# Forty-eight modulation weight tiles start earlier in the weight stream, and two paired reductions are drawn together

## The reference

```
mod   = silu(c)     @ w_ada + b_ada      # w_ada: 1024 x 6144
mod_c = silu(c_ctx) @ w_ada + b_ada      # only its first 2 x 1024 columns are used
sh1, sc1, g1, sh2, sc2, g2 = split(mod, 6)
h_lat = rms_norm(x, norm_mix) * (1 + sc1) + sh1
h_ctx = rms_norm(ctx, norm_mix) * (1 + csc1) + csh1
... gated linear attention, long convolution, x = x + g1 * (... @ w_out), MLP with sh2, sc2, g2
```

## Time and profile before

| | us |
|---|---|
| median of 3 runs | 1745.04 |
| lowest, highest | 1741.37, 1745.97 |
| the profiled execution | 1745.97 |
| its span | 1744.2 |
| TensorE busy | 1663.2 (95%) |
| VectorE, ScalarE, GpSimd busy | 769.8, 670.2, 710.0 |

### The profile page before, as it was taken

One profiled execution on the slowest core, in us unless ns is written; L12 is line 12 of the kernel. 1 busy time (PEld: TensorE's weight loads), 2 busy tenths in 40 slices (PEclk: granted clock), 3 DMA queues, 4 the chain that ended last, 5 costly groups with the idle time before them and its releaser, 6 DMA issues.

```text
span 1744.2 us, 19877 instructions
## 1 busy us (share of the span) xinstructions
PE 1663.2 (95%) x8208; PEld 1360.9 (78%) x8208; DVE 769.8 (44%) x1083; ACT 670.2 (38%) x966; POOL 710.0 (41%) x333
## 2 busy tenths in 40 slices
PE   5899999999999899999999999989989899999997
PEld 5787888788878687888887757678968688888885
DVE  4635997565654333443432645653262421111113
ACT  6543333333322342444444353236633443232322
POOL 4834343343434434333333325342412365464642
PEclk9999999999999899999999999999999999999999
DMA  6323344333435222323222222121201132222221
GB/s 224 133 84 127 140 160 153 140 130 111 142 120 179 77 93 87 96 96 97 96 89 98 76 106 75 47 84 65 73 1 48 61 109 97 97 97 97 97 85 48
DMA packets 51953, 175.98 MB, mean 101 GB/s; under 512 B 6284, under 2 KB 6924, under 8 KB 51352
## 3 DMA queue, kind: packets, MB, share of 16 engines
q1 hardware_dynamic: 51864, 174.73, 29.4%
HBM read 169.44 MB, written 2.12 MB: 98 GB/s over the span
## 4 chain that ended last, share of the span: by engine, by line
PE 84%; DVE 8%; ACT 4%; POOL 2%; issue 1%; DMA 1%; SPq 0%; DVEq 0%; ACTq 0%; POOLq 0%
PE banks L77 84%; DVE T L77 1%; ACT L77 1%; POOL wl L77 1%; DVE TM L77 1%; DVE X L77 1%; ACT R L77 1%; DVE Sc L77 1%; DVE ACC L77 0%; ACT wh L77 0%; DMA raw<-wst_dram 0%; DVE Y L77 0%; ACT T L77 0%; POOL HL L77 0%; DVE QG L77 0%
## 5 line engine op out<-in xcount | busy, mean ns | idle before, releaser
L77 POOL TENSOR_TENSOR wl<-raw,wh 128x1024 fp32r<-128x1024 f32 x246 | 610.2, 2488 | 672.4 <-ACT wh L77 672.4
L77 PE MATMUL banks<-HH,wh 128*128 128x512 f32 x1040 | 417.6, 402 | 16.1 <-ACT HH L77 9.0
L77 PE MATMUL banks<-HL,wh 128*128 128x512 f32 x1040 | 408.5, 393 | 0.1
L77 PE MATMUL banks<-HH,wl 128*128 128x512 f32 x1040 | 407.9, 392 | 0.0
L77 ACT ACTIVATE wh<-raw 128x1024 fp32r<-128x1024 f32 x246 | 257.4, 1053 | 380.8 <-PE banks L77 350.8
L77 PEld LDWEIGHTS banks<-HH,wh 128*128 128x128 f32 x1040 | 197.3, 190 | 64.4 <-issue 14.3
L77 PEld LDWEIGHTS banks<-HL,wh 128*128 128x128 f32 x1040 | 196.7, 189 | 44.6 <-DVE HL L77 2.3
L77 PEld LDWEIGHTS banks<-HH,wl 128*128 128x128 f32 x1040 | 197.3, 190 | 42.2 <-issue 2.6
L77 PE MATMUL banks<-wh,HH 128*128 128x256 f32 x448 | 128.7, 287 | 2.0 <-ACT QX L77 2.0
L77 PE MATMUL banks<-wl,HH 128*128 128x256 f32 x448 | 127.4, 284 | 0.0
L77 PE MATMUL banks<-wh,HL 128*128 128x256 f32 x448 | 127.4, 284 | 0.0
(11 more groups left out here) (285 smaller groups left out, 2553.8 us busy)
## 6 DMA issues: line engine op xcount, KB each, us to landing
raw<-wst_dram SPq DMA_DIRECT2D x294, 512.0 KB, 3.2
CB<-sums_dram SPq DMA_DIRECT2D x12, 256.0 KB, 3.0
D<-dec_dram SPq DMA_DIRECT2D x12, 256.0 KB, 2.6
X<-xT_dram SPq DMA_DIRECT2D x1, 2048.0 KB, 11.4
out_dram<-X SPq DMA_DIRECT2D x8, 256.0 KB
QS<-QX SPq DMA_DIRECT2D x24, 64.0 KB, 2.9
KSw<-KX SPq DMA_DIRECT2D x24, 64.0 KB, 2.0
MX<-memT_dram SPq DMA_DIRECT2D x2, 512.0 KB, 6.1
```

The costliest lines, as they stand in the source:

```text
L77: i = w[0](*w[1], **w[2])
```

## The change

The plan inserts two "ada" tiles after each of the four memory units. As there are 48 in all, every later one moves up, two per unit are given while p < 2 instead of p < 3, and the last stands four slots earlier. The c_ctx reduction of groups 0 and 1 is named for the same take as the other one.

```diff
--- before.py
+++ after.py
@@ -109,11 +109,13 @@
     plan.append(("f", "fox", 0, None))
     for cols in [4620, 5132 + 1536, 4876, 5132 + 1792]:
         pair("fox", 0, 8, (cols,))
+        ada(left.pop())
+        ada(left.pop())
     for p in range(6):
         for cols in (1536 + 256 * p, 256 * p, 3072 + 256 * p, 5132 + 256 * p):
             pair("fox", 0, 8, (cols,))
             ada(left.pop())
-            if p < 3:
+            if p < 2:
                 ada(left.pop())
     for n in range(4):
         for k in (12, 0, 4, 8):
@@ -314,7 +316,7 @@
             at_u = st["take"] + 4
             later.append((at_u, ada_reduce(targets[0][0], mod[:, 8 * g:8 * g + 8], P("bada", 8 * g, 8))))
             if g < 2:
-                later.append((at_u + 1, ada_reduce(targets[1][0], modc[:, 8 * g:8 * g + 8], P("bada", 8 * g, 8))))
+                later.append((at_u, ada_reduce(targets[1][0], modc[:, 8 * g:8 * g + 8], P("bada", 8 * g, 8))))
 
     def split_next():
         i = st["split"]
```

## The result

| | before | after |
|---|---|---|
| median of 6 runs each, us | 1745.51 | 1754.96 |
| lowest, highest | 1741.37, 1746.68 | 1748.91, 1759.13 |
| span of the profiled execution | 1744.2 | 1755.0 |

The ratio is 1.0053, 95% interval 1.0035 to 1.0072: slower by 0.53%. The forecast was 1752.0 with a range to 1757; the sign and the range held, the sum was too small.

The account below looks back on a forecast made before the run. The prediction took TensorE's own work and a few stalls to bound the kernel. Stall terms summed to +7.0 us on 1745.97, giving 1753.0 for the profiled execution and 1752.0 for the median, range 1745 to 1757.

Parts of the forecast that it names:

- The frame of the argument: Whole kernel: time is TensorE's own work and a few stalls; the edit adds no work, only changes stalls.
- What a `wl` costs a sum: VectorE's modulation sums beside GpSimd: the engines alternate, so a `wl` costs 2.15 us and an `OL` 1.1.
- The heads: Memory heads: group 0's sums delay the copies to `PT`; TensorE stalls 1.2, 1.2 and 2.6 us, 5.0 in all.
- Rival A: Memory heads: the sums slip into VectorE's idle time, +1.5 us in all, 1746.5 us; chance 0.30.
- `Kt`: Entry to the first head pair: VectorE's late `Kt` copy stalls TensorE 0.3 us.
- The reductions: First head pair: group 0's two reductions back to back wait for banks 6 and 7; stall 2.4 us.
- the high bound of 4.6 us: Upper bound on the stall at group 0's reductions: one `wl` in between, 2.15 us more.
- Group 1's pair: Second head pair: group 1's two reductions, with only two sums ahead, stall TensorE 0.6 us.
- `Vt`: Second head pair, at 246.69: TensorE's 1.27 us wait on `Vt` goes, −1.3 us.
- `Sc`: At 496.37: the 3.0 us wait on `Sc` keeps the same sums around it and stays.
- rival B: Stalls reaching 3.01 us, or a reduction meeting a `wl`, bring slow matmuls, 1.8 us each; about 1757 us; chance 0.17.
- Sum: All terms: 1.2 + 1.2 + 2.6 + 0.3 + 2.4 + 0.6 − 1.3 = +7.0 us.

Follow-up runs that it names:

- experiment 7: The kernel before with one modulation tile, instead of none, behind each of the four memory units: 1746.42 us, ratio 0.9998.
- experiment 3: The full change with group 0's c_ctx sums left out except the first, so half of `mod_c` is not computed: 1747.94 us, ratio 1.0020.
- experiment 8: The kernel before with head 11's transposes moved behind the second slot of the output projection, beside its attention product: 1743.23 us, ratio 0.9990.
- the later c_ctx reduction: The kernel before with the c_ctx reduction of groups 0 and 1 three takes after the other instead of one: 1743.45 us, ratio 0.9988.
- 4: The full change with ScalarE making both copies to `PT` in the first layer's four memory heads: 1749.80 us, ratio 1.0026.
- 1: Two kernels: new plan with the c_ctx reductions one weight slot later as before, 1749.15 us; kernel before with both reductions in the same slot, 1749.43 us.
- 2: The full change with the c_ctx reductions of groups 0 and 1 on banks 4 and 5 instead of 6 and 7: 1748.06 us, ratio 1.0020.
- 6: The full change with both reductions of groups 0 and 1 one weight slot later, still drawn together: 1778.66 us, ratio 1.0191.
- reductions alone: The kernel before, old plan, with the two reductions of groups 0 and 1 in the same weight slot: 1749.43 us, ratio 1.0028.
- the last kernel of 8: The kernel before with head 11's transposes later and the c_ctx reductions of groups 0 and 1 three slots behind the others: 1740.03 us, ratio 0.9972.

## Why the prediction came out as it did

- **The frame of the argument** (TensorE's own work and its stalls, no work added) held: every microsecond found is a wait, its restart, or matmuls at the lower clock.
- **What a `wl` costs a sum.** Predicted 2.15 us, seen 3.41 − 1.27 = 2.14; an `OL` 1.1 predicted, 2.33 − 1.28 = 1.05 seen. They alternate strictly. By the rule of the Trainium skill, page "SBUF — State Buffer", section "SBUF: two separate sides" (whoever starts first has the shared pair for the whole instruction), the sums would be 3.7 and 2.6 us long, an estimate from 2.40 and 1.30 us; the runs have the alternation, not the full lengths.
- **The heads.** Predicted 1.2 + 1.2 + 2.6 = 5.0; waited 0.89 + 0.54 + 1.72 = 3.15, and 3.9 with the restarts. The places were right, each wait 0.3 to 0.9 us shorter than I had reckoned, while the restarts, which the sum has at nothing, added 0.2 to 0.3 each. Rival A, sums in idle time, fell with the same rows; experiment 7 shows where it would have been true.
- **`Kt`.** 0.3 predicted, none. As `Kt` was on time, the lateness handed on to the reductions was less than supposed, and experiment 3, with VectorE on time, shows that it was not the point.
- **The reductions: the step that failed in size.** I took 2.4 us, on the ground that the last sum "starts just before a `wl`, as it did"; the wait was 4.17 us, and 5.8 with the slow matmuls and the restart. Before the sum had begun 0.27 us ahead of the `wl`; after it came 0.16 us behind. The `wl` follows the copy `wh`, and this waits for its tile's transfer. ScalarE's row before, and after:

```profile
162.48 1.06 ACT L77 ACTIVATE wh<-raw 128x1024 fp32r<-128x1024 f32 x1 [4.40 <-DMA raw<-wst_dram]
```

```profile
168.50 1.06 ACT L77 ACTIVATE wh<-raw 128x1024 fp32r<-128x1024 f32 x1 [5.02 <-DMA raw<-wst_dram]
```

  The transfer in turn needs a slot of the ring, which VectorE gives back with the last sum ahead of `Kt`. That sum ended at 158.64 and at 165.08, and SyncE issued at once:

```profile
158.67 0.81 SPq L77 DMA_DIRECT2D raw<-wst_dram  x2
```

```profile
165.11 1.28 SPq L77 DMA_DIRECT2D raw<-wst_dram  x3
```

  So a late VectorE moves the `wl` along with its own sums, and the order hangs on how long the transfer takes: `wh` began 3.84 us behind that sum's end before, and 3.42 after. The old plan has the dear order too, with VectorE on time. GpSimd and VectorE in the kernel with the later turn (experiment 8):

```profile
163.65 5.97 POOL L77 TENSOR_TENSOR wl<-raw,wh 128x1024 fp32r<-128x1024 f32 x2 [7.35 <-ACT wh L77]
```

```profile
163.95 3.42 DVE L77 SCALAR_TENSOR_TENSOR ada<-raw,scc,ada 128x1024 f32<-128x1024 f32 x1
```

  Of the five profiles with the old plan, two have the sum first (before and the later c_ctx reduction) and three the `wl`. Of the five with the new plan and VectorE's copy to `PT` ahead of the four sums, all have the `wl` first. "As it did" was thus one outcome of two in a single trace, and the row could not carry the term. What came is the case which I priced as the high bound of 4.6 us. Experiments 3 and 4 stand on the two sides of this race: 3.17 and 1.49 us waited.
- **Group 1's pair** 0.6 against 0.35 waited and 0.8 with the restart; **`Vt`** −1.3 against −1.27 waited and −1.6 with its restart; **`Sc`** unchanged, right.
- **The clock, rival B.** Its trigger was met: behind 4.17 us of idle eight transposes took 1.97 instead of 1.04 us and three matmuls up to 0.78, at a granted clock of 0.50 between 174 and 176 us. The tail was 1.4 us, near the 1.8 of the earlier trace rows. The rival's time of 1757 was too high because the heads' stalls stayed below 1.8 us and had no such tail.
- **Sum.** Predicted 7.0; by the rows 3.9 + 0 + 5.8 + 0.8 − 1.6 = 8.9, by the medians 9.4 (1.0053). The difference is nearly all in the reductions, 5.8 for 2.4, less 1.1 at the heads. That the total came out near 7.0 is in part luck, since these two errors have opposite signs; the range reached far enough because rival B stood in it, and B's conditions, a `wl` in a reduction and one stall above 3 us, are what happened.

The slowdown's cause is shown for the heads (experiments 1, 4, 7) and for the shared banks (1, 2, 6). That the 1.4 us tail is the clock is read from rows, not isolated by a run. That all five profiles of the new plan have the `wl` first, where the old plan has both orders, is not explained.

## What to carry to other kernels

Idle time of a helper engine is no room for more work unless it lies ahead of the instruction that the busy engine wants next: one tile fitted ahead of each copy here, two did not. Draw two reductions that share banks together only where nothing stands in the queue ahead of the first one's reader; the same pair cost 0.35 to 12 us by its place. Where two engines alternate, a change of a few tenths decides who goes first, so a term priced "as it was" there needs both prices in the sum. A single trace shows only one of them.

## What was not expected of the hardware

- **TensorE's clock was at the lower of its two levels behind every wait of 3 us or more looked at here.** Idle and what came behind it: 3.01 us, matmuls of 0.63 instead of 0.39 us; 3.17 us, six of 0.63; 3.65 us (reductions alone), seven of 0.63; 4.17 us, slow transposes and three matmuls; 7.14 us, sixteen matmuls of 256 columns at 0.41 instead of 0.28 us. The granted clock in those stretches was 0.50. Behind 1.70, 1.49 and 1.27 us there was none. The slow stretch did not grow with the wait: 4.8, 4.5, 5.0, 3.0 and 5.5 us from the restart to the first matmul of usual length. Nor is it the same behind one and the same wait: behind the 3.01 us on `Sc` the transposes took from 1.31 to 2.39 us in all, by the execution.
- **Behind the same wait of 2.5 us both outcomes occur.** At the start stage the kernels are alike, and the row there reads in the last kernel of 8 and in after:

```profile
73.02 0.38 PE L77 MATMUL banks<-wh,MH 128*128 128x256 f32 x1 [2.51 <-POOL wl L77]
```

```profile
71.47 0.58 PE L77 MATMUL banks<-wh,MH 128*128 128x256 f32 x1 [2.53 <-POOL wl L77]
```

Ten of the fourteen profiled executions have the slow form, of old and new plan both.
- **The first 90 us differ between executions.** The matmul that waits for `R` came between 86.80 and 90.20 us in the fourteen profiles, before any instruction that the edits move. For effects of some microseconds, times are to be counted from a common instruction behind it.
